# Seven products instead of eight for the last two chunks of four feed forward stages

## The reference

```python
def swiglu(x, w_in, w_out):
    a, b = jnp.split(x @ w_in, 2, axis=-1)
    return (jax.nn.silu(a) * b) @ w_out
    ...
        f = swiglu(rms_norm(h, g[4]), ffn2_w_in[l], ffn2_w_out[l])
        h = h + FFN_RES * rms_norm(f, g[5])
```

## Time and profile before

| | |
|---|---|
| median of three runs | 1417.25 us (1417.22 to 1417.32) |
| the profiled execution: its time, its span | 1416.94 us, 1415.1 us |
| PE busy | 1401.8 us (99%), 7327 matmuls |
| DVE busy | 956.5 us (68%) |
| ACT busy | 731.7 us (52%) |
| POOL busy | 160.1 us (11%) |
| DMA, mean over the span | 204 GB/s |

### The profile page before, as it was taken

One profiled execution on the slowest core, in us unless ns is written; L12 is line 12 of the kernel. 1 busy time (PEld: TensorE's weight loads), 2 busy tenths in 40 slices (PEclk: granted clock), 3 DMA queues, 4 the chain that ended last, 5 costly groups with the idle time before them and its releaser, 6 DMA issues.

```text
span 1415.1 us, 19090 instructions
## 1 busy us (share of the span) xinstructions
PE 1401.8 (99%) x7327; PEld 1147.2 (81%) x7327; DVE 956.5 (68%) x1307; ACT 731.7 (52%) x1050; POOL 160.1 (11%) x242
## 2 busy tenths in 40 slices
PE   9999999999999999999999999999999999999997
PEld 7888888688888888888878888888877788888886
DVE  6666567886676667665787757755568566786654
ACT  6444455564443445543665545445655634655542
POOL 1600010000000000000172100000542110011000
PEclk9999999999999999999999999999999999999999
DMA  9585755256876778868544688764845355588551
GB/s 318 199 253 198 262 203 207 68 171 207 251 242 215 231 228 265 252 210 264 187 150 148 203 210 256 255 211 140 238 160 197 121 178 179 171 242 211 178 209 59
DMA packets 234857, 288.24 MB, mean 204 GB/s; under 512 B 37076, under 2 KB 156672, under 8 KB 234768
## 3 DMA queue, kind: packets, MB, share of 16 engines
q1 hardware_dynamic: 232160, 281.48, 61.6%
q0 software_dynamic: 2208, 5.24, 1.8%
q10 hardware_dynamic: 400, 0.31, 0.1%
HBM read 282.80 MB, written 4.20 MB: 203 GB/s over the span
## 4 chain that ended last, share of the span: by engine, by line
PE 95%; DVE 2%; issue 1%; ACT 1%; POOL 0%; POOLq 0%; ACTq 0%; DVEq 0%
PE ps L706 29%; PE ps L709 28%; PE ps L707 28%; PE pst L974 1%; PE pst L1155 1%; DVE wlo L532 1%; PE pst L1468 1%; PE ps L813 0%; PE ps L812 0%; PE ps L811 0%; PE ps L1415 0%; ACT whi L521 0%; PE ps L679 0%; PE pst L1782 0%; PE pst L2355 0%
## 5 line engine op out<-in xcount | busy, mean ns | idle before, releaser
L532 DVE TENSOR_TENSOR wlo<-raw,whi 128x1024 fp32r<-128x1024 f32 (+2 forms) x468 | 558.2, 1224 | 257.7 <-ACT whi L521 255.9
L521 ACT ACTIVATE whi<-raw 128x1024 fp32r<-128x1024 f32 (+2 forms) x468 | 467.8, 1040 | 244.2 <-PE ps L709 97.4
L706 PE MATMUL ps<-whi,xh 128*128 128x512 f32 (+4 forms) x1406 | 551.5, 392 | 1.6 <-ACT xh L1013 0.6
L707 PE MATMUL ps<-wlo,xh 128*128 128x512 f32 (+4 forms) x1406 | 541.1, 385 | 0.0
L709 PE MATMUL ps<-whi,xl 128*128 128x512 f32 (+4 forms) x1406 | 532.7, 385 | 0.0
L706 PEld LDWEIGHTS ps<-whi,xh 128*128 128x128 f32 x1406 | 263.9, 188 | 60.6 <-issue 4.7
L709 PEld LDWEIGHTS ps<-whi,xl 128*128 128x128 f32 x1406 | 263.9, 188 | 53.6
L707 PEld LDWEIGHTS ps<-wlo,xh 128*128 128x128 f32 x1406 | 264.2, 188 | 49.8
L706 PE MATMUL ps<-whi,gh 128*128 128x512 f32 x440 | 172.0, 391 | 0.0
L707 PE MATMUL ps<-wlo,gh 128*128 128x512 f32 x440 | 171.2, 389 | 0.0
L709 PE MATMUL ps<-whi,gl 128*128 128x512 f32 x440 | 153.4, 389 | 0.0
(11 more groups left out here) (306 smaller groups left out, 956.0 us busy)
## 6 DMA issues: line engine op xcount, KB each, us to landing
raw<-in_ffn_w_in_dram SPq DMA_DIRECT2D x174, 512.0 KB, 5.3
raw<-in_ffn_w_out_dram SPq DMA_DIRECT2D x40, 1024.0 KB, 5.5
raw<-in_w_in_dram SPq DMA_DIRECT2D x26, 1024.0 KB, 4.8
adat<-in_w_ada_dram SPq DMA_DIRECT2D x96, 256.0 KB, 2.8
raw<-in_hyb_w_in_dram SPq DMA_DIRECT2D x10, 1024.0 KB, 5.1
raw<-in_gla_w_in_dram SPq DMA_DIRECT2D x10, 1024.0 KB, 5.2
raw<-in_w_ffn_down_dram SPq DMA_DIRECT2D x10, 1024.0 KB, 5.0
raw<-in_w_ffn_gate_dram SPq DMA_DIRECT2D x18, 512.0 KB, 3.9
```

Of the source, the lines that this page charges most:

```text
L521: e.activation(split_of(whi, j), raw_of(j), ACT.Copy).then_inc(*whi_made.up(j))
L532: e.tensor_tensor(split_of(wlo, j), raw_of(j), split_of(whi, j).bitcast(F32), ALU.subtract).then_inc(*wlo_made.up(j))
L706: e.matmul(ps[:, 0:n], a, whi_of(j, k), start=first and k == 0, stop=False)
L707: last = e.matmul(ps[:, 0:n], a, wlo_of(j, k), start=False, stop=False)
```

## The change: what it does

Stages 2, 3 and 5 join stage 7 in the form with seven products. In all four, the pair is now chunks 9 and 10 (`PAIR = 9`), the first product p1 stands after chunk 2, and the last, p4, after chunk 8, directly ahead of the down product. Chunk 8 is now the one that is turned alone (`alone`), ahead of the first sub of the down product, and the pair is turned in the down product's fourth sub, which takes its tokens in another order at its start. Products with their own buffers (all but p2) carry no tile of `mod`; the groups of eight tiles start 9 or 10 units apart instead of 10, and send, read and fold stand one unit earlier behind a group. For stages 2, 3 and 5 the row of gains of the closing norm is loaded at the down product's first unit, after p4's weights are split, since p1, p5, p6 and p4 use its buffer.

```diff
-        STRASSEN = (7,)
-        PAIR = 8
+        STRASSEN = (2, 3, 5, 7)
+        PAIR = 9
...
             if st in STRASSEN:
-                return (0, 1, "p1", 2, "p2", 3, "p5", 4, "p6", 5, "p3", 6, "p7", 7, "p4", 10)
+                return (0, 1, 2, "p1", 3, "p2", 4, "p5", 5, "p6", 6, "p3", 7, "p7", 8, "p4")
             return tuple(range(11))
...
-        ada_units = [u for st in (0, 2, 3, 5) for u in range(U0[st] + (8 if st == 0 else 0), U0[st + 1])]
+        ada_units = [u for st in (0, 2, 3, 5) for u in range(U0[st] + (8 if st == 0 else 0), U0[st + 1]) if u not in home]
...
         for c in range(12):
+            i = min(10 * c, c * (len(ada_units) - 13) // 11)
             for k in range(8):
-                ada_tiles[ada_units[10 * c + k]] = c, k
-            ada_sent[ada_units[10 * c + 11]] = c
-            ada_read[ada_units[10 * c + 12]] = c
-            ada_summed[ada_units[10 * c + 13]] = c
+                ada_tiles[ada_units[i + k]] = c, k
+            ada_sent[ada_units[i + 10]] = c
+            ada_read[ada_units[i + 11]] = c
+            ada_summed[ada_units[i + 12]] = c
...
                 held.append(i)
+                if key[1] in STRASSEN and i == 0:
+                    continue
+                if key[1] in STRASSEN and i == 1:
+                    one(held.pop(0), 1)
...
+        def alone(st):
+            return PAIR - 1 if st in STRASSEN else 10
...
             def at(i):
-                if i == 2:
+                if i == (0 if st in STRASSEN else 2):
                     pe_hid(e, st)
+                if st in STRASSEN and i == 3:
+                    pe_hid_two(e, st, PAIR)
...
-        COMBINE = {2: "p1", 5: "p6", 7: "p7"}
+        COMBINE = {3: "p1", 6: "p6", 8: "p7"}
...
-                    if st in STRASSEN and (c, i) == (2, 1):
+                    if st in STRASSEN and (c, i) == (3, 1):
                         act_sx(e, st)
...
-                if i == 2:
-                    act_ghi(e, st, 10)
+                if i == (0 if st in STRASSEN else 2):
+                    act_ghi(e, st, alone(st))
+                if st in STRASSEN and i == 0:
+                    act_silu_pair(e, st, 0)
+                    act_silu_pair(e, st, 1)
...
-                if st in STRASSEN and c == 1:
+                if st in STRASSEN and c == 2:
                     dve_sx(e, st)
-                if st in STRASSEN and c == 2:
+                if st in STRASSEN and c == 3:
                     dve_sx_lo(e, st)
...
             pool_open(e, 2)
+            pool_strassen(e, 2)
             pool_open(e, 3)
+            pool_strassen(e, 3)
             pool_gla(e)
             pool_open(e, 5)
+            pool_strassen(e, 5)
```

More of the change, by code:

```diff
@@ L1126, in dve_gate_pair, with turn_of @@
                                    ).then_inc(*gated.up(st, PAIR, tok))
-        def turn_of(c):
+        def turn_of(st, c):
+            if st in STRASSEN:
+                return PAIR - 1 if c == PAIR - 1 else PAIR if c >= PAIR else c - c % 2
             return c if c == 10 else c - c % 2
+        def alone(st):
+            return PAIR - 1 if st in STRASSEN else 10
         def pe_hid(e, st):
-            ps = tb.next(("hid", st, 10), (glo_made, st, 10))
+            c = alone(st)
+            ps = tb.next(("hid", st, c), (glo_made, st, c))
             for done in tb.freed:
                 e.wait_ge(*done)
-            e.wait_ge(*gated.at(st, 10, 1))
+            e.wait_ge(*gated.at(st, c, 1))
             for j in range(2):
@@ L1140, in pe_hid @@
                                        hid[0][:, tok * 512 + j * P:tok * 512 + (j + 1) * P], ident)
-            last.then_inc(*hid_turned.up(st, 10))
+            last.then_inc(*hid_turned.up(st, c))
         def pe_hid_two(e, st, c):
@@ L1166, in act_ghi @@
             e.wait_ge(*hid_turned.at(st, c))
-            if c == 10:
-                e.activation(gh[:, 5120:5632], tb.of("hid", st, c)[:, :], ACT.Copy).then_inc(*ghi_made.up(st, c))
+            if c == alone(st):
+                e.activation(gh[:, c * 512:(c + 1) * 512], tb.of("hid", st, c)[:, :], ACT.Copy).then_inc(*ghi_made.up(st, c))
             else:
@@ L1173, in dve_glo @@
             e.wait_ge(*ghi_made.at(st, c))
[L1174 to L1175 removed]
+            if c == alone(st):
+                e.tensor_tensor(gl[:, c * 512:(c + 1) * 512], tb.of("hid", st, c)[:, :], gh[:, c * 512:(c + 1) * 512].bitcast(F32), ALU.subtract
                                 ).then_inc(*glo_made.up(st, c))
@@ L1193, in pe_ffn_in @@
                     pe_product(e, st, c, base)
-                    if c == "p4":
-                        pe_hid_two(e, st, PAIR - 2)
                     continue
                 def at(i, c=c):
-                    if c % 2 == 0 and i == (3 if st in STRASSEN and c == 10 else 2):
+                    if c % 2 == 0 and i == 2:
                         pe_hid_two(e, st, c - 2)
@@ L1253, in act_ffn @@
                 act_begin(e, JD[st] + i)
-                if i == 2:
-                    act_ghi(e, st, 10)
+                if i == (0 if st in STRASSEN else 2):
[3 more added lines that the diff above has]
+                    act_silu_pair(e, st, 1)
+                if st in STRASSEN and i == 3:
+                    act_ghi(e, st, PAIR)
         def dve_ffn(e, st):
@@ L1273, in dve_ffn @@
                     dve_begin(e, JC[st, c] + i)
-                    if st in STRASSEN and i == 3 and c in (5, 7):
+                    if st in STRASSEN and i == 3 and c in (6, 8):
                         dve_combine(e, st, COMBINE[c])
@@ L1285, in dve_ffn @@
                 dve_begin(e, JD[st] + i)
-                if i == 2:
-                    dve_glo(e, st, 10)
+                if i == (0 if st in STRASSEN else 2):
+                    dve_glo(e, st, alone(st))
+                if st in STRASSEN and i == 0:
+                    dve_gate_pair(e, st, 0)
+                    dve_gate_pair(e, st, 1)
+                if st in STRASSEN and i == 3:
+                    dve_glo(e, st, PAIR)
         hyb_gate = sig("hyb_gate")
```

18 lines of the change are left out of this document (5 added, 13 removed).

## The result

The changed kernel is slower: 1424.91 us (1424.08 to 1426.32, 4 runs) beside 1417.24 us before, a ratio of 1.0057 (95% interval 1.0040 to 1.0075). The forecast was 1414.0 with a range to 1417.3 and 0.06 for slower; it was wrong. The profiled execution took 1424.08 us with a span of 1422.3, 7.2 us more than before. With 8.1 us of matmuls gone, some 15 us of new idle or slow time must be on PE.

What follows compares the result with a forecast made beforehand. PE's list of matmuls, busy for 99% of the span, was taken as the bound: 1416.94 - 8.1 + 3.0 + 1.5 + 0.3 = 1413.6, given as 1414.0 us against the median, with a range from 1410.2 to 1417.3.

Steps and rivals of the forecast that it cites:

- The matmuls, -8.1: Stages 2, 3 and 5: 36 fewer matmuls on PE, 12 per stage, saving 8.1 us.
- p2 in stage 2, 2.4 us: PE waits 2.4 us at p2 for ACT's copy of p1, behind the split of a unit delayed by a tile's addition.
- The 0.6 us for gates before chunk 4: Stage 2: chunk 4 starts in the bank freed by DVE's first gate, at +19.35 against +18.7, another 0.6 us.
- The entry of stage 5, 1.5 us: Five fold operations now stand between DVE's addition and the scaling of new tokens, costing 1.5 us, all on the path.
- has none at chunk 3's units, so there that unit is issued at about +7.3, and PE waits for nothing: Stage 5 at p2: no tile at chunk 3's units, so chunk 4's first unit goes out in time, no wait.
- The start of the down product, 0.3 us: ACT's split of a unit ahead of silu: 0.3 us for all four stages, between 0 and 4 x 1.5 us.
- Stages 3 and 5 otherwise 0: No tile delays chunk 4's first unit at p2 in stages 3 and 5, so PE waits for nothing there.
- DVE's 96 of 116 us: Estimate of DVE's work per changed stage, 16 us more than before; DVE stays below PE on average.
- POOL's transfers, 0: p7's weights in stage 7 land with 8.4 us left, so POOL's transfers were priced at nothing.
- the 20.7 from which it decides: Time from issue to split of p7's second half, 20.7 us, past which the slower rival's mechanism decides.
- The slower rival: Accumulating POOL transfers become late at p7's second half; PE waits 6.9 us more, 1421 us; chance 0.06.
- More of the points are late: Rival, chance 0.24: stages 3 and 5 lose 1.5 us each at p2 or the down product, 1417.0 us.

Runs made afterwards that it cites:

- the pair of runs without `mod`: Changed kernel with gates' transfer moved, and kernel before, both without w_ada's tiles, additions, sends and folds in stages 2, 3 and 5: 1407.82 and 1415.59 us.
- the last version: Changed kernel with gates' transfer moved, silu first, two folds and p6's sum later, mod's tiles re-placed (none at p2, stage 2): 1408.83 us, ratio 0.9941.
- the run with three edits: Changed kernel with the gates' transfer in stage 4, silu of the pair ahead of the split, and two folds later: 1414.87 us, ratio 0.9987.
- two edits taken singly: Changed kernel with only two folds moved later, 1423.52 us; changed kernel with only silu of the pair ahead of the split, 1424.15 us.

## Why the prediction was wrong, by its own steps

**The matmuls, -8.1: right.** Stage 3 shows -2.8, the pair of runs without `mod` -7.8 in all, the last version -8.0.

**p2 in stage 2, 2.4 us: right in place, chain and size, 2.3 us.** ACT's timeline after, at the predicted place:

```profile
358.22 1.06 ACT L522 ACTIVATE whi<-raw 128x1024 fp32r<-128x1024 f32 x1 [3.41 <-DMA raw<-in_ffn_w_in_dram]
359.19 0.58 ACT L828 ACTIVATE ps<-ps 128x512 f32<-128x512 f32 x1
```

The unit was issued at +8.5 and split at +14.5, against 8.3 and 14.3. The 0.6 us for gates before chunk 4 did not come, though the first gate ended at +19.3 as counted: the matmuls behind the wait ran slow, 1.7 us, for which there was no term, and PE came later than the gate. In the run with three edits, where they did not run slow, PE waits 0.3 us there.

**The entry of stage 5, 1.5 us: right, 1.48.** DVE and PE after, against the earlier trace rows: the five fold operations stand between the addition and the scaling.

```profile
792.70 0.74 DVE L619 SCALAR_TENSOR_TENSOR adaacc<-adat,scol,adaacc 128x512 f32<-128x512 f32 x1
793.36 0.42 DVE L626 TENSOR_TENSOR fold<-fold 128x256 f32<-128x256 f32 x1
...
794.80 0.16 DVE L635 TENSOR_TENSOR modc<-modc,vcol 128x4 f32<-128x4 f32 x1
794.88 1.29 DVE L1003 TENSOR_TENSOR work<-pst,vcol 128x512 f32<-128x512 f32 x2
...
796.38 0.47 PE L707 MATMUL ps<-whi,xh 128*128 128x512 f32 x1 [1.48 <-ACT xh L1018]
```

**Stage 5 "has none at chunk 3's units, so there that unit is issued at about +7.3, and PE waits for nothing": this step failed.** It priced the landing of every unit with the 6.0 us of one row of stage 2. What else is on the queue was asked for tiles and sends only. "That unit" is chunk 4's first; it was issued at 828.94, 2.0 us before p1, and did no harm. The one that went out at +7.4 was chunk 4's second, right behind the gates' transfer, and it landed in 12.1 and 13.2 us. The transfer stood in the trace of before; the loads behind it landed in 10.7 and 11.9 us there, and nobody waited. The run with it moved shows 7.0 us for it, over 40% of all that was lost.

**The start of the down product, 0.3 us: right in place, too small.** I named stage 3 and its four sends and bounded the stage at 1.5 us; it was 1.15, and 1.4 with what follows. The other stages lost nothing there. The bound of 1.5 us did not hold: with the gates' transfer moved PE waited 2.87 us at the same place.

**"Stages 3 and 5 otherwise 0", and the folds looked at in one place only.** Of the folds that the change moves, the forecast priced the one at stage 5's entry. The one ahead of chunk 1's gates cost 0.9 us in stage 2 (run with two folds later), and p6's sum, which waits for POOL with gates behind it, cost up to 1.8 us once PE ran on time. In stage 7 of the kernel before, from which the forecast was read, PE has no wait behind that sum.

**DVE's 96 of 116 us: too much.** The windows show 89 to 91 us; no term of the sum rests on it.

**POOL's transfers, 0: right for p7.** Stage 5, the latest: issue on POOL and the split of the last half on ACT.

```profile
886.46 2.43 POOL L558 DMA_DIRECT2D work<-in_ffn_w_in_dram  x2 [11.39 <-DVE wlo L533]
...
900.51 1.06 ACT L522 ACTIVATE whi<-work 128x1024 fp32r<-128x1024 f32 x1 [2.42 <-DMA work<-in_ffn_w_in_dram]
```

These are 14.1 us against the 20.7 from which it decides. The slower rival thus had its sign right and its mechanism wrong. The rule of the Trainium skill, *SBUF — State Buffer*, "SBUF: two separate sides", that DVE can lock GpSimd out of a shared port pair, is not what happened to p3's transfer in stage 5: it was issued while DVE stood idle for 5.2 us, and landed late all the same, its first half in 7.8 us. With the 4-byte transfer moved away it took 4.0 us, and DVE was busy for 3.9 of them.

```profile
848.23 1.50 POOL L560 DMA_DIRECT2D work<-in_ffn_w_in_dram  x2 [21.30 <-DVE sxl L606]
...
853.12 2.36 DVE L533 TENSOR_TENSOR wlo<-raw,whi 128x1024 fp32r<-128x1024 f32 x2 [5.19 <-ACT whi L522]
```

**The chances.** "More of the points are late" had 0.24 and ended at 1417. It was the case that came, but each late point was priced at 1.5 us, and slow matmuls behind a wait had no price. A kernel with no wait at all has room on one side only.

## What to carry to other kernels

Before denser work is put at a place, list every transfer that the queue issues there, the small ones above all, and read how long its neighbours take to land; a slow transfer that nobody waited for is in the trace already. When PE is at 99%, a fix is to be judged by its gap in the trace and not by the total alone: two edits taken singly gained 1.4 and 0.8 us, within the noise, though their gaps were gone; both are part of the last version, which gained 16. And one trace is one execution: the wait at p2 measured 2.0 to 2.7 us in six kernels that do not differ there. And work that only fills holes, like `mod`, has places of its own: its sends, reads and folds moved by one unit, without any other change, cost 3.4 us.

## What the runs showed of the hardware

One transfer of 4 KB in 1024 elements of 4 bytes took 10.5 us, and for some eight of them the core moved about 50 GB/s or less beside the 250 to 380 behind it; the loads that SP issued behind it waited along, and what POOL issued at its end met the backlog. The Trainium skill, *DMA: Bandwidth & Descriptors*, "Why small descriptors are slow (HBM only)", explains a fixed overhead per packet and per descriptor; the trace agrees in kind: three reads of 64 KB in elements of 512 bytes, issued 1.0 to 1.8 us ahead of it, landed in 2.5 to 2.7 us; a fourth, issued 0.5 us ahead, took 10.1. Moved to a stretch of stage 4 with little traffic (96 GB/s) the transfer took 10.7 us, in the last version 8.5 us, and no wait of PE followed.

TensorE's clock fell behind some waits and not behind others. Windows of the changed kernel behind the wait of 3.9 us in stage 5, and shortly later (PEclk is the third column from the end; 0.50 is 1.2 GHz of 2.4):

```profile
866.80:869.40 2.60, 2.60 (x6) 2.10 (x7) 2.60 (x4) 1.20 (x2) 0.00 (x0) 0.50 0.00 0
870.20:872.00 1.80, 1.80 (x10) 1.48 (x9) 1.80 (x2) 0.69 (x1) 0.00 (x0) 1.00 0.49 126
```

Matmuls started every 0.43 us there, 7 of them, 1.5 us lost. The same place in stage 2, in two kernels: the run with three edits, which waited there for 2.4 us, in the window behind the wait

```profile
360.00:362.00 2.00, 2.00 (x11) 1.53 (x9) 1.78 (x2) 0.92 (x3) 0.00 (x0) 1.00 0.99 327
```

and the run with p6's sum moved, which waited for 2.2 us:

```profile
360.00:362.00 2.00, 2.00 (x6) 1.59 (x5) 2.00 (x5) 0.05 (x1) 0.00 (x0) 0.50 1.03 334
```

The longer wait left the clock at full, the shorter halved it; and behind the wait of 2.87 us in stage 3, in the run with the gates' transfer moved, the clock was 1.00 too. So the length of the wait alone does not decide; what does stays open. In these kernels a wait of 2 us and more is best priced as itself or as itself and 1.4 to 1.7 us.
